# Thirty-six modulation units inside the first feed-forward, and nine row buffers for x

## The chip, the cores and the metric

The kernel runs on one core of one Trainium2 chip. The metric is the device time of one execution in microseconds (us), and lower is better.

## The reference, cut to what matters

One layer of a streaming encoder on 1152 tokens (1024 of a prompt, 8 sequences of 16 sample tokens), model width 1024, in 32-bit floating point. All sub-layers are modulated: a vector of eleven groups of 1024 numbers is computed for each of the nine sequences from its conditioning vector.

```python
def ada_mod(c, w, b, n):
    m = jax.nn.silu(c) @ w + b                 # c is (9, 1024) in all, w is (1024, n * 1024)
    return m.reshape(c.shape[0], n, D_MODEL)

def ffn_sublayer(x, mod, base, g, w1, w3, w2):
    h = modulate(rms_norm(x, g), mod[:, base], mod[:, base + 1])
    gate = 1 + mod[:, base + 2][:, None, :]
    return x + MACARON_W * gate * swiglu(h, w1, w3, w2)
```

The layer is `ffn_sublayer` with groups 0 to 2, the token mixing with groups 3 to 5, `ffn_sublayer` with groups 6 to 8, and a final norm with two more groups (9 and 10, from the weights `w_ada_f`). The feed-forward width is 2816. So the first feed-forward needs groups 0 and 1 (shift and scale) before its first product and group 2 (gate) before its first output is added to x; the other eight are needed after it.

## The kernel before, in words

The program is written engine by engine with counted semaphores; nothing is scheduled for it. SyncE (SP) issues the loads, TensorE (PE) multiplies, VectorE (DVE), ScalarE (ACT) and GpSimd (POOL) do the rest. Each engine's list of work is in the order in which the code writes it.

**Setup (lines 336 to 573).** The modulation weights are 22 halves of 512 columns (`ADA_HALVES`), each 2 MB, loaded into four buffers `ada_w`. For a half, PE does eight products that accumulate over the 1024 rows (`ada`, line 465): the stationary operand is the conditioning `cT[:, k, :]` (128 by 9), the moving one 512 columns of weights, the result is 9 partitions by 512. DVE copies it to `mod_rows` (`copy_rows`), PE turns it so that channels lie on the partitions (`turn_rows`, line 473, four small products), and DVE adds the bias into `mods` (`add_bias`). A product in plain 32-bit floats is two TensorE instructions in the trace, so a half is 16 rows of line 465 and 8 of line 473. Between the halves the nine tiles of 128 rows of x come through two buffers `x_rows` and are transposed (`turn_x`, line 456; DVE's copy is line 515). After half 15 the small states are turned, and `minus_sums` (line 303) runs over the past log gates.

**Norm (lines 575 to 678).** For three chunks of 384 tokens: squares on ACT, the sum over channels on PE (`norm_sum`, line 594), root on ACT, reciprocal (line 604) and product with x (line 612) on DVE, the modulation on DVE (line 623) and ACT (line 633), and the split of the result into a high part (`acts_hi`, ACT, line 641) and a low part (`acts_lo`, DVE, line 646), each in the format fp32r. The first norm waits for all of setup (`x_set_up`: `mod_final` 7 and `past_stored`).

**Feed-forward (`ffn_sync` to `ffn_vector`, lines 682 to 813).** Eleven pairs, each of 256 of the 2816 columns. A pair loads three blocks of 1 MB (of w1, w3, w2) into the two buffers `w_raw`; ACT and POOL split each into `w_hi` and `w_lo`. PE then does six groups of 48 products of 384 columns (banks 0 to 3, three products for each pair of operands, `mm3`), and 24 output groups of six products into banks 4 to 7; DVE adds each of the 24 to x with the gate (`add_gated`). Between the groups ACT computes the SiLU (`gated`) and DVE its product (`u_f`, line 806).

```python
            for c in range(NC):
                for d in range(KT):
                    eng.wait_ge(sem("y_free"), it * 24 + c * 8 + d - 4 + 1 + CREDIT)
```

## Time and profile before

| | |
|---|---|
| median of 3 runs | 3716.43 us (3714.55 to 3716.44) |
| span of the profiled execution | 3719.7 us |
| time around that span | none is shown beside it |
| TensorE busy | 3549.7 us, 95% of the span |
| TensorE clock, mean over the span | 0.980 of full |
| VectorE, ScalarE, GpSimd busy | 34%, 24%, 19% |
| moved from and to memory | 343.11 MB, 92 GB/s over the span |

The profile is one execution, seen by the hardware profiler. Its span runs from the first to the last instruction. In the rows below, times are microseconds unless marked ns. PE is TensorE's products, PEld its weight loads, SPq the queue that issues the loads. L465 is line 465 of the kernel. Products on TensorE are pipelined, so the distance from one start to the next says what an instruction takes, and the busy time of one is longer.

### The profile page before, as it was taken

The numbers are of one execution on the slowest core, as the hardware profiler recorded it, in microseconds if no ns is written. First come the engines' busy times: TensorE is split into PE (matmuls) and PEld (weight loads), VectorE is DVE, ScalarE is ACT, GpSimd is POOL, SyncE is SP. The second block draws the span as 40 slices with busy tenths as digits, with TensorE's granted clock in tenths as the row PEclk, the third lists the DMA queues.
The fourth block names the chain that finished last, engine by engine and source line by source line (L and its number), as shares of the span: only waits on it lengthen the run. The fifth ranks groups of instructions, "written<-read, shape, count | busy, mean of one in ns | idle before, by whom it ended". The sixth has DMA issues, their size and how long they took to land.

```text
span 3719.7 us, 53696 instructions
## 1 busy us (share of the span) xinstructions
PE 3549.7 (95%) x21007; PEld 3244.3 (87%) x21007; DVE 1276.8 (34%) x2798; ACT 909.3 (24%) x1360; POOL 705.8 (19%) x282
## 2 busy tenths in 40 slices
PE   8889999999999999999998998888999999999997
PEld 2269999999988999999998888444998999999997
DVE  1242322223256232232413766333324232223225
ACT  0031111111134232322323665222013111111112
POOL 0012322232201111111122221000111322223220
PEclk9999999999999999999999999999999999999999
DMA  8721111111111313131443333887510111111101
GB/s 303 240 76 34 45 40 50 34 42 37 57 51 61 106 65 106 48 117 54 151 146 109 89 92 82 276 279 254 194 56 28 35 44 56 34 34 45 50 18 51
DMA packets 245498, 343.11 MB, mean 92 GB/s; under 512 B 56093, under 2 KB 164053, under 8 KB 245138
## 3 DMA queue, kind: packets, MB, share of 16 engines
q1 hardware_dynamic: 218962, 308.42, 25.9%
q10 hardware_dynamic: 26432, 33.18, 2.4%
q8 instruction: 81, 1.33, 0.1%
q14 instruction: 23, 0.19, 0.0%
HBM read 293.54 MB, written 48.01 MB: 92 GB/s over the span
## 4 chain that ended last, share of the span: by engine, by line
PE 89%; DVE 3%; DMA 3%; issue 2%; ACT 2%; SPq 2%; DVEq 0%; ACTq 0%
PE psum L269 24%; PE psum L273 24%; PE psum L272 24%; PE psum L465 4%; PE psum L1412 3%; DMA kn<-k_t 2%; PE psum L1642 2%; PE psum L1392 1%; PE psum L1629 1%; PE psum L990 1%; DVE h_f L612 1%; PE psum L1379 1%; PE psum L1673 1%; PE psum L594 1%; SPq L1596 1%
## 5 line engine op out<-in xcount | busy, mean ns | idle before, releaser
L269 PE MATMUL psum<-acts_hi,w_hi 128*128 128x384 f32 x4032 | 1372.1, 340 | 29.4 <-issue 18.5
L273 PE MATMUL psum<-acts_hi,w_lo 128*128 128x384 f32 x4032 | 1359.8, 337 | 0.0
L272 PE MATMUL psum<-acts_lo,w_hi 128*128 128x384 f32 x4032 | 1359.8, 337 | 0.0
L259 POOL TENSOR_TENSOR w_lo<-w_raw,w_hi 128x2048 fp32r<-128x2048 f32 x106 | 494.1, 4670 | 1821.4 <-ACT w_hi L253 1821.4
L269 PEld LDWEIGHTS psum<-acts_hi,w_hi 128*128 128x128 f32 x4032 | 761.9, 189 | 35.6 <-issue 30.8
L272 PEld LDWEIGHTS psum<-acts_lo,w_hi 128*128 128x128 f32 x4032 | 761.8, 189 | 3.3
L273 PEld LDWEIGHTS psum<-acts_hi,w_lo 128*128 128x128 f32 x4032 | 761.5, 189 | 0.0
L806 DVE TENSOR_TENSOR u_f<-psum,gated 128x384 f32<-128x384 f32 x132 | 73.6, 558 | 994.2 <-ACT gated L761 994.2
L829 DVE SCALAR_TENSOR_TENSOR x<-psum,mods,x 128x384 f32<-128x384 f32 (+1 forms) x552 | 314.9, 570 | 194.6 <-PE psum L273 194.6
L253 ACT ACTIVATE w_hi<-w_raw 128x2048 fp32r<-128x2048 f32 x106 | 200.5, 1910 | 644.4 <-PE psum L269 606.0
L269 PE MATMUL psum<-u_hi,w_hi 128*128 128x384 f32 x1056 | 357.6, 339 | 0.0
L273 PE MATMUL psum<-u_hi,w_lo 128*128 128x384 f32 x1056 | 357.1, 338 | 0.0
L272 PE MATMUL psum<-u_lo,w_hi 128*128 128x384 f32 x1056 | 357.0, 338 | 0.0
L784 POOL TENSOR_TENSOR u_lo<-u_f,u_hi 128x384 fp32r<-128x384 f32 x132 | 134.2, 1016 | 870.4 <-ACT u_hi L763 870.4
L761 ACT ACTIVATE gated<-psum 128x384 f32<-128x384 f32 x132 | 64.9, 491 | 841.8 <-PE psum L273 841.8
L272 PEld LDWEIGHTS psum<-u_lo,w_hi 128*128 128x128 f32 x1056 | 198.5, 188 | 0.3
L269 PEld LDWEIGHTS psum<-u_hi,w_hi 128*128 128x128 f32 x1056 | 198.5, 188 | 0.3
L273 PEld LDWEIGHTS psum<-u_hi,w_lo 128*128 128x128 f32 x1056 | 198.5, 188 | 0.0
L465 PE MATMUL psum<-ada_w,cT 128*9 128x512 f32 x352 | 158.8, 605 | 14.0 <-DMA ada_w<-in_w_ada 14.0
L1412 PE MATMUL psum<-vh,pT 128*128 128x64 f32 x1152 | 146.9, 274 | 8.2 <-DVE acts_lo L1533 5.7
L1412 PEld LDWEIGHTS psum<-vh,pT 128*128 128x128 f32 x1152 | 140.8, 194 | 12.6 <-DVE acts_lo L1533 8.6
L1045 ACT ACTIVATE st<-psum 128x384 f32<-128x384 f32 x120 | 58.7, 490 | 337.6 <-PE psum L273 336.6
(224 smaller groups left out, 2880.5 us busy)
## 6 DMA issues: line engine op xcount, KB each, us to landing
w_raw<-in_ffn_w SPq DMA_DIRECT2D x66, 1024.0 KB, 5.4
ada_w<-in_w_ada SPq DMA_DIRECT2D x18, 2048.0 KB, 9.6
kc<-in_cache_k SPq DMA_DIRECT2D x16, 2048.0 KB, 10.3
vc<-in_cache_v SPq DMA_DIRECT2D x16, 2048.0 KB, 8.5
w_raw<-in_w_in SPq DMA_DIRECT2D x28, 1024.0 KB, 5.2
sp<-sample_bias SPq DMA_DIRECT2D x128, 65.0 KB, 6.7
ada_w<-in_w_ada_f SPq DMA_DIRECT2D x4, 2048.0 KB, 15.6
kf<-k_t SPq DMA_DIRECT2D x32, 256.0 KB, 4.6
```

What stands on the lines that cost most here:

```text
L253: eng.activation(w_hi[st][:], w_raw[raw][:], ACT.Copy).then_inc(sem("w_hi_done"), 1)
L259: eng.tensor_tensor(w_lo[st][:], w_raw[raw][:], w_hi[st][:].bitcast(F32), ALU.subtract).then_inc(sem("w_lo_done"), 1)
L269: pass1 = eng.matmul(out, whi, ahi, start=first, stop=False)
L272: eng.matmul(out, whi, alo, start=False, stop=False)
L273: return eng.matmul(out, wlo, ahi, start=False, stop=last)
L465: last = eng.matmul(ps[4 + slot % 2][0:NSEQ, :], cT[:, k, :], ada_w[slot][:, k, :], start=(k == 0), stop=(k == KT - 1))
L761: eng.activation(gated[n % 2][:], ps[2 * (n % 2)][:, 0:CH], ACT.Silu).then_inc(sem("gated_ready"), 1)
L784: eng.tensor_tensor(u_lo[:, t, tokens_of(c)], u_f[n % 2][:], u_hi[:, t, tokens_of(c)].bitcast(F32), ALU.subtract).then_inc(sem("u_lo_done" ...
L806: eng.tensor_tensor(u_f[n % 2][:], ps[2 * (n % 2) + 1][:, 0:CH], gated[n % 2][:], ALU.mult).then_inc(sem("u_free"), 1)
L829: last = eng.scalar_tensor_tensor(xt[:, d, t0:t0 + cp], bank[:, 0:cp], mods[:, gate, d, 0:1], xt[:, d, t0:t0 + cp], ALU.mult, ALU.add)
L1412: last = eng.matmul(ps[6 + k % 2][:, 0:HD], pT[k % 2][:, 128 * kb:128 * kb + 128], vh[hh][:, kb, :], start=(kb == 0), stop=(kb == qi))
L1642: last = eng.matmul(psum[rows, base + 512 * bk:base + 512 * bk + 512], qd[g][:, p, :], kTs[p % 2][:, 512 * bk:512 * bk + 512], start=True, ...
```

## The change

Of the 22 halves, four stay in front of the first feed-forward (groups 0 and 1). The other eighteen become 36 units of 256 columns, four in each of the first nine of the eleven pairs. A unit is loaded into `w_raw[1]`, the buffer that the w3 block uses in between. Its product is made from four column groups of the array: row block k goes to the output partitions of group k % 4, with the conditioning padded with zeros to 32 columns, and the turn sums the four groups. All nine tiles of x have a row buffer of their own and are loaded before the weights; the norm's sums stand ahead of the modulation products. The feed-forward's output groups use banks 4, 5 and 6 in place of 4 to 7 in the first feed-forward (bank 7 is for the units). The three `log1p` parts and the sums over the past log gates now stand after the norm. Several semaphores are merged.

```diff
+    FIRST = 4
+    ADA_PAIRS = 9
+    N_UNITS = 4 * ADA_PAIRS
+    def ada_product(eng, out, weights, n):
+        for k in range(KT):
+            g = k % 4
+            last = eng.matmul(out[32 * g:32 * g + 32, 0:n], cT[:, k, :], weights[:, k, :], start=(k < 4),
+                              stop=(k >= 4), skip_group_check=True)
+        last.then_inc(sem("ada_full"), 1)
+    def ada_turn(eng, out, rows, tiles):
+        for t in range(tiles):
+            last = eng.matmul(out[:, NSEQ * t:NSEQ * t + NSEQ], rows[:, 128 * t:128 * t + 128], row_sum,
+                              start=True, stop=True)
+        last.then_inc(sem("mod_turned"), 1)
...
     def setup_tensor(eng):
...
+        for c in range(NC):
+            norm_sum(eng, 0, c)
...
+        product(0)
+        product(1)
+        turn(0)
+        product(2)
+        turn(1)
+        turn(2)
+        product(3)
+        turn(3)
+
+    def setup_rest_tensor(eng):
         eng.wait_ge(sem("state_loaded"), 48)
...
+        eng.wait_ge(sem("past_summed"), 3)
...
+    def ffn1_sync(eng):
+        def unit(i, u, source):
+            if u == 0:
+                eng.wait_ge(sem("w_lo_done"), B_FFN1 + i * 3 + 1 + 1 + CREDIT)
+            eng.wait_ge(sem("ada_full"), i * 4 + FIRST + u)
+            eng.dma_start(w_raw[1][:].rearrange("p (k n) -> p k n", k=KT), source).then_inc(sem("ada_unit_loaded"), 16)
+        def pair(i, view, col, first=False):
+            ffn_load(eng, 0, i, 2)
+            if first:
+                past_store(eng)
+            unit(i, 0, view[:, :, ds(col, 256)])
+            ffn_load(eng, 0, i + 1, 0)
+            for u in range(1, 4):
+                unit(i, u, view[:, :, ds(col + 256 * u, 256)])
+            eng.wait_ge(sem("ada_full"), i * 4 + FIRST + 4)
+            ffn_load(eng, 0, i + 1, 1)
...
+    Y_BANKS = (3, 4)
...
     def ffn_tensor(eng, f):
...
+        def ada_step(i, n):
+            if n >= 1:
+                eng.wait_ge(sem("mod_rows_ready"), i * 4 + FIRST + n)
+                eng.wait_ge(sem("mod_ready"), i * 4 + FIRST + n - 1)
+                eng.wait_ge(sem("y_free"), i * 24 + CREDIT)
+                ada_turn(eng, ps[4][:, 0:2 * NSEQ], mod_part, 2)
+            if n < 4:
+                eng.wait_ge(sem("ada_unit_loaded"), i * 64 + 16 * n + 16)
+                ada_product(eng, ps[7], w_raw[1][:].rearrange("p (k n) -> p k n", k=KT), 256)
...
                     last.then_inc(sem("a_full"), 1)
+                    if ada and n < 5:
+                        ada_step(i, n)
...
-                    eng.wait_ge(sem("y_free"), it * 24 + c * 8 + d - 4 + 1 + CREDIT)
+                    eng.wait_ge(sem("y_free"), it * 24 + c * 8 + d - Y_BANKS[f] + 1 + CREDIT)
...
     def ffn_vector(eng, f):
+        def ada_step(i, n):
+            if n >= 1:
+                add_bias(eng, ps[4][:, 0:2 * NSEQ], i * 4 + FIRST + n - 1, i + 2, 2 * n - 2, 2,
+                         ds(i * 8 + 4 * FIRST + 2 * n - 2, 2))
+            if n < 4:
+                eng.wait_ge(sem("ada_full"), i * 4 + FIRST + n + 1)
+                eng.wait_ge(sem("mod_turned"), i * 4 + FIRST + n)
+                eng.tensor_copy(mod_part[:], ps[7][:, 0:256]).then_inc(sem("mod_rows_ready"), 1)
...
     def ffn_blocks_ahead(eng, f):
...
+        if f == 0:
+            eng.wait_ge(sem("ada_full"), 3)
         ffn_split_hi(eng, f, 0, 0)
+        if f == 0:
+            eng.wait_ge(sem("ada_full"), FIRST)
         ffn_split_hi(eng, f, 0, 1)
```

Where things stand in a row now. First TensorE from its first product to the feed-forward, in the kernel before, with one pass of the loop over the halves cut out (`ident,x_rows` are the transposes of x, `ident,mod_rows` the turns, `sq,ones` the norm's sums):

```order
L446 MATMUL psum<-ident,c_rows 128x9 x8
L465 MATMUL psum<-ada_w,cT 9x512 x8
...
L456 MATMUL psum<-ident,x_rows 128x128 x8
...
L465 MATMUL psum<-ada_w,cT 9x512 x8
L473 MATMUL psum<-ident,mod_rows 128x9 x8
L594 MATMUL psum<-sq,ones 128x384 x24
```

The same stretch of TensorE in the changed kernel, whole (`cols` holds the matrix that sums the four groups, `states` the padded conditioning):

```order
L479 MATMUL psum<-ident,c_rows 128x9 x8
L493 MATMUL psum<-ident,x_rows 128x128 x32
L486 MATMUL psum<-ident,vec_rows 128x88
L487 MATMUL psum<-ident,vec_rows 128x96
L493 MATMUL psum<-ident,x_rows 128x128 x40
L645 MATMUL psum<-sq,ones 128x384 x24
L455 MATMUL psum<-ada_w,states 32x512 x16
L462 MATMUL psum<-cols,mod_rows 128x9 x4
...
L526 MATMUL psum<-ident,h_rows 128x64
L528 MATMUL psum<-ident,conv_rows 128x96 x2
L533 MATMUL psum<-ident,past_rows 128x128 x8
```

The norm's sums (24 products) moved from behind the last half to ahead of the first; the past rows, which stood between halves, are now the last thing before the feed-forward.

Then VectorE of the changed kernel, from the last bias of setup to the first product of the feed-forward (`h_f` is modulated by line 682, `lam_t` are the `log1p` parts, line 309 the sums over the past log gates):

```order
L546 SCALAR_TENSOR_TENSOR mods<-mods,params 128x72
L682 TENSOR_SCALAR h_f<-h_f,mods 128x384 x5
L706 TENSOR_TENSOR acts_lo<-h_f,acts_hi 128x8x384
L682 TENSOR_SCALAR h_f<-h_f,mods 128x384 x5
L706 TENSOR_TENSOR acts_lo<-h_f,acts_hi 128x8x384
...
L601 TENSOR_TENSOR wfl_lo<-wfl_raw,wfl_hi 128x128
L603 COPY h<-psum 128x64
L604 COPY conv_state<-psum 128x192
L309 SCALAR_TENSOR_TENSOR past_rows<-ones,psum 128x512
L309 SCALAR_TENSOR_TENSOR past_rows<-ones,past_rows,psum 128x512
```

TensorE waits for the last of these (`past_summed` 3) before the first product of the feed-forward.

Last, TensorE inside a pair, at the end of the second of its six groups in the first pass of the loop:

```order
L277 MATMUL psum<-acts_hi,w_lo 128x384
...
L462 MATMUL psum<-cols,mod_part 128x9 x2
L807 REGISTER_ALU
L455 MATMUL psum<-w_raw,states 32x256 x8
L817 REGISTER_ALU
L273 MATMUL psum<-acts_hi,w_hi 128x384
```

The turn of the unit before and the product of this unit stand between two groups of 48; in the kernel before the groups follow each other with nothing between.

## Rows read from the trace of the kernel before

**Rows 1.** The page: the span, and busy time of each engine.
```profile
span 3719.7 us, 53696 instructions
...
PE 3549.7 (95%) x21007; PEld 3244.3 (87%) x21007; DVE 1276.8 (34%) x2798; ACT 909.3 (24%) x1360; POOL 705.8 (19%) x282
```
**Rows 2.** Busy time by stretch: from:to length, engines, clock, DMA share, GB/s.
```profile
0.00:217.40 217.40, 191.58 (x621) 62.09 (x621) 37.02 (x88) 10.48 (x14) 10.81 (x14) 0.98 0.73 255
217.40:242.50 25.10, 17.45 (x48) 9.89 (x48) 14.00 (x10) 15.60 (x11) 0.00 (x0) 0.84 0.00 0
242.50:321.50 79.00, 78.97 (x438) 78.98 (x439) 41.62 (x63) 22.26 (x25) 21.25 (x9) 0.97 0.13 41
321.50:397.20 75.70, 75.70 (x434) 75.70 (x433) 20.30 (x47) 11.68 (x16) 19.92 (x9) 1.00 0.13 42
```
**Rows 3.** Chain that ended last, 0 to 330: start, length, what.
```profile
5.66 7.99 DMA ada_w<-in_w_ada
...
31.20 6.96 PE psum L465 x16
38.17 0.98 PE psum L473 x8
...
234.00 2.05 DVE h_f L623 x5
236.13 2.77 ACT acts_hi L641
238.93 3.37 DVE acts_lo L646
```
**Rows 4.** Transfers, 10 to 20, by stretch as in rows 2.
```profile
10.00:20.00 10.00, 6.21 (x9) 1.13 (x10) 0.00 (x0) 0.31 (x1) 0.33 (x1) 1.00 1.05 395
```
**Rows 5.** Groups by line, 0 to 260: count, busy, mean ns, idle before.
```profile
L594 PE MATMUL psum<-sq,ones 128*128 128x384 f32 x48 | 17.4, 528 | 4.2 <-ACT sq L588 4.2
...
L515 DVE COPY x<-psum 128x512 f32 (+1 forms) x18 | 11.5, 686 | 2.8 <-PE psum L456 2.8
...
L604 DVE RECIPROCAL psum<-psum 128x384 f32<-128x384 f32 x3 | 7.7, 2561 | 10.7 <-ACT psum L600 10.7
...
L612 DVE TENSOR_TENSOR h_f<-x,psum 128x3072 f32<-128x3072 f32 x2 | 6.7, 3350 | 0.0
```
**Rows 6.** States, past sums and log1p on VectorE, by stretch as in rows 2.
```profile
171.70:178.70 7.00, 5.03 (x17) 1.67 (x18) 5.05 (x19) 0.21 (x1) 0.00 (x0) 1.00 1.05 388
```
**Rows 7.** TensorE in order of time, sample attention: start, length, group.
```profile
2419.16 0.26 PE L1652 MATMUL psum<-kn,qd 128*32 128x16 f32 x8
2419.35 1.20 PE L1662 MATMUL psum<-ident,sp 128*128 128x128 f32 x9
...
2421.59 1.95 PE L1673 MATMUL psum<-vc,spT 128*32 128x128 f32 x64 [1.05 <-DVE spT L1759]
2423.48 0.42 PE L1673 MATMUL psum<-vn,spT 16*32 16x128 f32 x8
```
**Rows 8.** TensorE in order of time, plain 32-bit products inside the projections.
```profile
1176.46 1.45 PE L990 MATMUL psum<-xc,bd 128*128 128x384 f32 x4
1177.45 0.63 PE L269 MATMUL psum<-acts_hi,w_hi 128*128 128x384 f32 x1
1177.92 0.34 PE L272 MATMUL psum<-acts_lo,w_hi 128*128 128x384 f32 x1
```
**Rows 9.** VectorE in order of time, a pair of the first feed-forward.
```profile
314.45 0.29 DVE L826 TENSOR_TENSOR s_tmp<-psum,mods 128x128 f32<-128x128 f32 x1 [0.17 <-PE psum L273]
...
346.46 0.56 DVE L806 TENSOR_TENSOR u_f<-psum,gated 128x384 f32<-128x384 f32 x1 [7.75 <-ACT gated L761]
354.85 0.56 DVE L806 TENSOR_TENSOR u_f<-psum,gated 128x384 f32<-128x384 f32 x1 [7.83 <-ACT gated L761]
```
**Rows 10.** Landing times of 1 MB blocks: inside the feed-forward, then 0 to 250.
```profile
DMA to landing us min/median/max: 4.7/5.4/8.0
...
w_raw<-in_ffn_w SPq DMA_DIRECT2D x3, 1024.0 KB, 12.4
```

More of the change, by code:

```diff
@@ L83, in program @@
     w_raw = [sb(ctx, f"w_raw{n}", [128, 2048]) for n in range(2)]
+    adaf = ExitStack()
+    ada_w = [sb(adaf, f"ada_w{n}", [128, KT, 512]) for n in range(2)]
+    adaf.close()
     w_hi = [sb(ctx, f"w_hi{n}", [128, 2048], F32R) for n in range(2)]
@@ L213, in program @@
     zf.close()
-    CONSTS = 4
+    CONSTS = 5
     NORMS_BEFORE = 3
@@ L336, in setup_sync @@
     def setup_sync(eng):
+        eng.dma_start(c_rows[0:1, :], a["c_prompt"]).then_inc(sem("c_loaded"), 16)
+        eng.dma_start(c_rows[1:NSEQ, :], a["c_sample"]).then_inc(sem("c_loaded"), 16)
+        xp = a["x_prompt"][0].rearrange("(m p) d -> m p d", p=128)
+        for tile in range(T // 128):
+            source = xp[tile] if tile < TP // 128 else a["x_sample"].rearrange("s t d -> (s t) d")
+            eng.dma_start(x_rows[tile][:], source).then_inc(sem(f"x_rows_loaded{tile // 3}"), 16)
+            if tile == 3:
+                load_vectors(eng)
@@ new lines, in load_half @@
+        def load_half(h, slot):
+            eng.dma_start(ada_w[slot][:], w_ada_v[:, :, 512 * h:512 * h + 512]).then_inc(sem(f"ada_loaded{slot}"), 16)
+        for h in range(3):
+            load_half(h, h)
+        ffn1_loads_ahead(eng)
+        eng.wait_ge(sem("ada_full"), 1)
+        load_half(3, 0)
+        eng.dma_start(state_rows[0][:], a["state_rglru"].rearrange("l s (r c) -> (l s r) c", c=128)).then_inc(sem("state_loaded"), 16)
+        conv_src = a["state_conv"].rearrange("l s j (r c) -> (l s j r) c", c=128)
@@ L455, in turn_x @@
                 for k in range(4):
-                    last = eng.transpose(ps[2 * slot + half][:, 128 * k:128 * k + 128],
-                                         x_rows[slot][:, 512 * half + 128 * k:512 * half + 128 * k + 128], ident[:])
+                    last = eng.transpose(ps[tile % 2 * 2 + half][:, 128 * k:128 * k + 128],
+                                         x_rows[tile][:, 512 * half + 128 * k:512 * half + 128 * k + 128], ident[:])
                 last.then_inc(sem("x_turned"), 1)
-        def ada(h, slot, loads):
-            eng.wait_ge(sem(f"ada_loaded{slot}"), 16 * loads)
-            for k in range(KT):
-                last = eng.matmul(ps[4 + slot % 2][0:NSEQ, :], cT[:, k, :], ada_w[slot][:, k, :],
-                                  start=(k == 0), stop=(k == KT - 1))
-            last.then_inc(sem("ada_full"), 1)
@@ L487, in setup_tensor, with product, turn @@
-        turn_x(0, TP // 128, TP // 256 + 1)
+        eng.wait_ge(sem("params_ready"), 1)
+        for c in range(NC):
+            norm_sum(eng, 0, c)
+        def product(h):
+            eng.wait_ge(sem(f"ada_loaded{h % 3}"), 16 * (h // 3 + 1))
+            if h >= 2:
+                eng.wait_ge(sem("mod_rows_ready"), h - 1)
+            ada_product(eng, ps[START_BANKS[h % 2]], ada_w[h % 3], 512)
+        def turn(h):
+            eng.wait_ge(sem("mod_rows_ready"), h + 1)
+            if h >= 1:
+                eng.wait_ge(sem("mod_ready"), h)
+            ada_turn(eng, ps[4][:, TURN_AT], mod_rows[h % 2], 4)
@@ L495, in setup_tensor @@
         for half in range(2):
[L496 removed]
             for k in range(4):
[L498 removed]
+                last = eng.transpose(ps[1 + half][:, 128 * k:128 * k + 128], past_rows[:, 4 * half + k, :], ident[:])
             last.then_inc(sem("states_turned"), 1)
[L500 to L503 removed]
+        eng.wait_ge(sem("past_summed"), 3)
@@ L538, in setup_vector, with copy_rows @@
-        move_x(0, TP // 128)
+                eng.tensor_copy(x[:, 4 * half:4 * half + 4, 128 * tile:128 * tile + 128],
+                                ps[tile % 2 * 2 + half][:].rearrange("p (k n) -> p k n", k=4)).then_inc(sem("x_moved"), 1)
+        for c in range(NC):
+            norm_inverse(eng, 0, c)
+            norm_times_inverse(eng, 0, c)
+        def copy_rows(h):
+            eng.wait_ge(sem("ada_full"), h + 1)
+            if h >= 2:
+                eng.wait_ge(sem("mod_turned"), h - 1)
+            eng.tensor_copy(mod_rows[h % 2][:], ps[START_BANKS[h % 2]]).then_inc(sem("mod_rows_ready"), 1)
@@ L650, in norm_scalar @@
     def norm_scalar(eng, n, x_ready):
-        for c in range(NC):
-            x_ready(eng, c)
-            norm_square(eng, n, c)
-            if c >= 1:
-                norm_root(eng, n, c - 1)
+        if n > 0:
+            for c in range(NC):
+                x_ready(eng, c)
+                norm_square(eng, n, c)
+                if c >= 1:
+                    norm_root(eng, n, c - 1)
         if n < 3:
@@ new lines, in ffn1_loads_ahead @@
+    def ffn1_loads_ahead(eng):
+        ffn_load(eng, 0, 0, 0)
+        ffn_load(eng, 0, 0, 1)
+    def ffn1_sync(eng):
[14 more added lines that the diff above has]
+            ffn_load(eng, 0, i + 1, 1)
+        pair(0, w_ada_v, 2 * D, first=True)
+        with eng.Fori(1, NMOD - 4) as i:
+            pair(i, w_ada_v, i * D + 2 * D)
+        with eng.Fori(0, 2) as i:
+            pair(i + (NMOD - 4), w_adaf_v, i * D)
+        with eng.Fori(ADA_PAIRS, FF_PAIRS - 1) as i:
+            ffn_load(eng, 0, i, 2)
+            ffn_load(eng, 0, i + 1, 0)
+            ffn_load(eng, 0, i + 1, 1)
+        ffn_load(eng, 0, FF_PAIRS - 1, 2)
@@ L1976, in _ @@
         setup_tensor(eng)
-        for c in range(NC):
-            norm_sum(eng, 0, c)
+        setup_rest_tensor(eng)
         ffn_tensor(eng, 0)
```

384 lines of the change are left out of this document (195 added, 189 removed).

## The prediction

> **What bounds the kernel now.** I read the page first: TensorE is busy for 95% of the span [rows 1]. A share is an average, so the second view is the busy time by stretch [rows 2]. For 217.4 us TensorE computes the modulation, then 25.1 us of norm follow with no transfer at all, and the first product of the feed-forward stands at 242.5. A pair then takes 75.7 us (the first one 79.0), with TensorE full and the transfers at 0.13. The third view, the chain of waits [rows 3], shows what fills the front: a half is 6.96 us of products (16 instructions, 0.435 us each for 512 columns, or 0.85 ns a column) and 0.98 us of turns, and 22 x 7.94 = 175 us of the 217 are that. The result has nine rows, so this is TensorE time spent on streaming weights past a nearly empty array. A half of 2 MB needs 5.3 us at 395 GB/s [rows 4], less than its 7.94: the front is bound by TensorE, not by memory.
>
> So two questions decide: how much earlier the feed-forward starts, and what a unit costs inside pairs where TensorE has no idle time.
>
> **What a product of four column groups costs.** The sample attention already has this form [rows 7]: 64 instructions of 128 columns, four groups in turn, have their successor 1.89 us later, 29.5 ns each, where 0.85 ns a column would give 109. They run beside each other, 3.7 times faster. A unit is 8 products, 16 instructions of 256 columns: 16 x 218 / 3.7 = 0.94 us. One of the four halves in front takes 1.88 us. The turn of a unit is four instructions at 0.98 / 8 = 0.12 [rows 3]: 0.49 us.
>
> The Trainium skill (TensorE: Matmul & The Clock Gate, the table of measured packing) gives 2.38 times for three column groups. Scaled to four that would be 3.2, an estimate from that page, and 5 us more over the 36 units. The measured row decides, since it is this form on this engine.
>
> **The start, added up.** Loads: the first 2 MB took 7.99 us from issue [rows 3], of which 5.3 are the transfer, so 2.7 us are latency. Three tiles of x (1.6 MB, 4 us) land at about 8, all nine (12 us) at 16. VectorE copies a tile in 2 x 0.686 [rows 5]: from 8.5, nine tiles and the parameters end at 21. The three sums take 17.4 us on TensorE [rows 5] and run from 20.6 to 38. VectorE then is the one that is late. Its reciprocal and product are 2.56 + 3.35 a chunk [rows 5], from 28.5 for three chunks to 46.4, and only then does it copy the first half (0.69 for this form, as for x) at 47.1. Halves 0 and 1 were multiplied by 41.5, so TensorE waits 5.6 us. From 47.1 come, in turn, four turns (4 x 1.0), two products (2 x 1.9, some of it at the lower clock, which TensorE also had after its wait in the norm, mean 0.84 [rows 2]; 5.3 together), two copies (1.4) and the small steps: 58.4. Half 3 is loaded when product 0 is done, at 40 + 8 = 48, before it is needed.
>
> Then chunk 0 is modulated, rounded and subtracted: 2.05 + 2.77 + 3.37 [rows 3], with the hops to 67.2, and chunk 1 behind it to 76. Before, TensorE started right behind chunk 0. Now it waits for the past sums, which stand behind chunk 1 on VectorE: their whole group was 5.05 us busy [rows 6], here 5.7 with ScalarE's logarithm in it. **The feed-forward starts at 81.7 and not at 242.5: 160.8 us earned.** For the bounds: 72, if VectorE keeps closer to the loads and the hops are short; 95, if the small loads (64-byte pieces) or the table loads of ScalarE come late.
>
> **What the pairs pay.** Four units are 4 x (0.94 + 0.49) = 5.7 us a pair, and all of it lies on the path, since TensorE is full there [rows 2]. On top comes the break in the stream, five a pair. Four plain 32-bit instructions of 384 columns between fp32r products [rows 8] move the stream by 1177.92 - 1176.46 - 0.17 = 1.29, of which 4 x 384 x 0.85 ns = 1.30 are their own streaming: a break costs nothing. By the second row alone it costs 0.3 (0.47 to the next start instead of 0.17). I take 0.15, between them: 45 x 0.15 = 6.8, with 0 and 13.5 kept as ends. Nine pairs: 51.5 + 6.8 = 58.
>
> The Trainium skill (TensorEngine Tiling (Array Packing), Tiling Modes) speaks against this change: a change of the tiling mode drains the engine. The row says less. Eight column-group products and the full-width ones behind them start 0.19 us apart [rows 7], no room for a drain of any size. By the rule, an estimate from it with what a product has in flight (0.34 long, 0.17 apart) for 72 switches, it would be 12 us more.
>
> **What waits, pair by pair.** A unit is loaded when the product before is done. The groups of 48 are 8.39 us apart [rows 9] (354.85 - 346.46), so with the turn there are 9.0 us. A 1 MB block in the same 1 KB pieces lands after 5.4 us, at most 8.0 [rows 10]: no wait. SyncE's queue is strict, and the load for w1 of the next pair stands ahead of unit 1. It waits for GpSimd's split of w2, which is done 6 us into the pair, so it holds nothing up. w3 of the next pair now starts after unit 3, some 40 us into the pair, lands at 46, and is split after the last group at 59: late by nothing. On VectorE a step adds a copy and a bias, about 0.7 us, where it sat idle for 7.8 [rows 9]. Three output banks for four: at its busiest VectorE still waits 0.17 us for TensorE at each output group [rows 9], so two banks in flight are enough. Nothing is paid.
>
> In the first pair VectorE modulates chunk 2 behind the second group and waits for ScalarE in it; the copy of unit 1 comes about 2.3 us after TensorE wants it. That is 2.5 us, once. The store of the past sums (0.5 MB) has 10 us to land before ScalarE's first SiLU needs its space.
>
> **The sum.** 58 + 2.5 - 160.8 = -100 against the span of 3719.7. The median of the runs is 3.3 us below that span and I take the difference to stay: 3716.4 - 100.0 = 3616 us. Ends: start 72 and free breaks give -170.5 + 51.5 = -119, 3597. Start 95, breaks of 0.3 and 8 us of waits in the first pairs give -147.5 + 65 + 8 = -74.5, 3642.
>
> **Rivals.**
> - *Units land late.* Each of 27 loads (units 1 to 3) has 9.0 us. In setup, with other loads in the queue, 1 MB took 12.4 us [rows 10]. At 10 us: 27 x 1.3 = 35, so 3652. At 12.4: 27 x 3.7 = 100, so 3717. For it: the traffic inside a pair grows from 3 to 7 MB. Against it: the share is 0.13 now, and the loads come one at a time. 7% for some of it, 1% for all.
> - *The column groups don't overlap* beside fp32r work with 256 columns. Then a unit's product is 3.49 us and not 0.94: 36 x 2.55 = 92. Four halves in front cost 5.1 us more each, less the 5.6 idle: 15. With breaks of 0.3: 7. Together 114 - 100 = +14, 3730, slower than before. The point from which it decides: slower when a unit costs over 4.4 us in all. Against it stands the row of the sample attention. 4%.
> - *The start does not shrink as the sum says:* VectorE's chain or the small loads put it beyond 100. Then 18 us and more are lost, 3635 to 3650. 10%, inside the range.
> - *The change doesn't do what it says,* with SyncE's queue holding the units behind a block that waits for the pair's end: then each pair would stall for tens of us. The order of the queue shows no such block. Under 1%.
>
> **How the numbers follow.** 78% for the forecast as added up, 10% for the late start, 8% for late units, 4% for groups one after another. The range 3597 to 3652 takes in the ends of the sum, the late start and the landing of 10 us; some 12% lies outside. A measurement of this kernel can tell 0.2%, 7.4 us, from no change. Slower by more is the 4% rival, within 0.2% is the full landing time, 2% with its neighbours, and faster is the rest.
>
> **What would show it.** In the profile of the changed kernel: the first feed-forward product at 72 to 95, with TensorE waiting on VectorE twice before it (copy of the first half, past sums); the three sums ahead of the modulation; steps of 16 instructions in 0.9 to 1.0 us in the units; pairs 0 to 8 at 81 to 84 us, pairs 9 and 10 still at 75.7; no wait on a unit's load; and everything behind the first feed-forward as long as it was. Wrong would be: unit products at 3.5 us, waits of TensorE on `w_raw`, pairs over 86, or a start past 100.

## The result and the profile after

| | before | after |
|---|---|---|
| median of the runs on the same chip | 3715.49 us (3712.62 to 3716.44, 4) | 3626.96 us (3621.44 to 3627.85, 4) |
| span of the profiled execution | 3719.7 us | 3625.7 us |
| first product of the first feed-forward | 242.5 | 84.1 |
| first `u_f` of the first feed-forward | 254.14 | 95.52 |
| last `u_f` of the first feed-forward | 1052.56 | 951.45 |
| first to last product with `vc` (sample attention) | 2352.9 to 2605.5 | 2253.2 to 2512.7 |

The ratio is 0.976, 95% interval 0.9746 to 0.9774: 88.5 us faster, 94.0 by the spans. 3616 was forecast.

The page of the changed kernel, as in [rows 1]:
```profile
span 3625.7 us, 54412 instructions
...
PE 3439.9 (95%) x21295; PEld 3232.4 (89%) x21295; DVE 1283.6 (35%) x2835; ACT 910.2 (25%) x1360; POOL 704.2 (19%) x283
```
TensorE has lost 109.8 us of work and the same share of a shorter span is left. Busy time by stretch, columns as in [rows 2] (the stretches are setup with the norm, pair 0, pair 1, and two pieces of the first two):
```profile
0.00:83.90 83.90, 43.87 (x237) 28.43 (x237) 52.77 (x65) 30.89 (x29) 11.16 (x15) 0.81 0.63 204
83.90:171.30 87.40, 84.52 (x500) 80.87 (x501) 27.48 (x54) 17.17 (x20) 20.24 (x9) 0.93 0.32 103
171.30:252.70 81.40, 81.40 (x514) 78.75 (x513) 22.20 (x55) 11.63 (x15) 19.93 (x9) 1.00 0.28 90
60.00:80.00 20.00, 0.00 (x0) 0.00 (x0) 13.95 (x22) 12.51 (x14) 1.99 (x1) 0.50 0.09 37
116.00:130.00 14.00, 12.96 (x71) 11.67 (x71) 2.05 (x6) 0.52 (x1) 1.00 (x1) 0.76 0.24 76
```
In front TensorE now is busy for half the time, and for the last 20 us not at all: a chain on VectorE and ScalarE has taken its place as the bound. A steady pair is 81.4 with TensorE full, at a DMA share of 0.28. The first pair is 5.8 longer.

The front, from the chain of waits (start, length, what):
```profile
41.40 3.35 DVE h_f L660
44.75 0.61 DVE mod_rows L576
45.41 1.88 PE psum L462 x8
...
57.57 4.52 DVE mods L546
62.12 2.04 DVE h_f L682 x5
64.24 2.77 ACT acts_hi L701
...
72.44 2.77 ACT acts_hi L701
75.23 3.36 DVE acts_lo L706
...
82.39 1.29 DVE past_rows L309
```
L576 is the copy of the first half behind all three norm chunks, L309 the past sums. L546 turns a scale into its final form; the same operation takes 0.23 us in experiments 7 and 10, and here it lasted 4.5. TensorE in order of time: first setup, then in pair 0 the turn of unit 1 with the product of unit 2, and one such step of pair 1:
```profile
20.53 15.65 PE L645 MATMUL psum<-sq,ones 128*128 128x384 f32 x48
36.11 3.64 PE L455 MATMUL psum<-ada_w,states 128*32 128x512 f32 x32
...
84.13 0.68 PE L273 MATMUL psum<-acts_hi,w_hi 128*128 128x384 f32 x1 [25.20 <-DVE past_rows L309]
...
117.04 1.03 PE L462 MATMUL psum<-cols,mod_part 128*128 128x9 f32 x4 [2.65 <-DVE mod_part L929]
118.00 1.94 PE L455 MATMUL psum<-w_raw,states 128*32 128x256 f32 x16
...
211.24 0.51 PE L462 MATMUL psum<-cols,mod_part 128*128 128x9 f32 x4
211.68 1.07 PE L455 MATMUL psum<-w_raw,states 128*32 128x256 f32 x16
```
A steady turn takes 0.44 us (211.68 - 211.24) and a unit's product about 1.07. In pair 0 TensorE waits 2.65 us for the copy of unit 1 and then runs at twice these times. VectorE in order of time shows the pair's rhythm, one group of 48 products with turn and product each, then the output groups:
```profile
192.24 0.56 DVE L938 TENSOR_TENSOR u_f<-psum,gated 128x384 f32<-128x384 f32 x1 [8.57 <-ACT gated L884]
...
202.06 0.56 DVE L938 TENSOR_TENSOR u_f<-psum,gated 128x384 f32<-128x384 f32 x1 [8.62 <-ACT gated L884]
...
211.96 0.56 DVE L938 TENSOR_TENSOR u_f<-psum,gated 128x384 f32<-128x384 f32 x1 [8.62 <-ACT gated L884]
```
9.90 us where [rows 9] had 8.39: a unit with its turn and all its breaks costs 1.51. The output groups of the kernel after, and in the second block of rows of the kernel before:
```profile
154.99 0.62 DVE L971 SCALAR_TENSOR_TENSOR x<-psum,mods,x 128x384 f32<-128x384 f32 x1 [0.42 <-PE psum L277]
156.03 0.62 DVE L971 SCALAR_TENSOR_TENSOR x<-psum,mods,x 128x384 f32<-128x384 f32 x1 [0.42 <-PE psum L277]
```
```profile
300.72 0.62 DVE L829 SCALAR_TENSOR_TENSOR x<-psum,mods,x 128x384 f32<-128x384 f32 x1 [0.44 <-PE psum L273]
301.78 0.62 DVE L829 SCALAR_TENSOR_TENSOR x<-psum,mods,x 128x384 f32<-128x384 f32 x1 [0.44 <-PE psum L273]
```
They stand 1.040 us apart, before 1.056 (means over the first feed-forward, and the same in the second, which the change does not touch). That is 24 x 0.016 = 0.38 us a pair for nothing that was asked for.

**Where 94.0 us come from.** To the first `u_f` -158.6; pair 0 +11.6 (87.20 for 75.64); the next eight +46.2 (81.43 for 75.66); the last stretch -0.2. To the last `u_f` that is -101.1. Behind it the program lost 7.1: 2674.2 us from there to the end, before 2667.1. Most of that lies in the sample attention. First the transfers into `kc`, by the page of after, then of before (KB each, median us to landing):
```profile
kc<-in_cache_k SPq DMA_DIRECT2D x16, 2048.0 KB, 10.9
```
```profile
kc<-in_cache_k SPq DMA_DIRECT2D x16, 2048.0 KB, 10.3
```
Then busy time from the first to the last product with `vc`, of after, of before, and of the kernel of experiment 12, columns as in [rows 2]:
```profile
2253.20:2512.70 259.50, 216.93 (x2092) 124.87 (x2092) 89.94 (x221) 63.52 (x116) 0.00 (x0) 0.93 0.87 261
```
```profile
2352.90:2605.50 252.60, 215.28 (x2090) 122.22 (x2092) 89.94 (x221) 63.46 (x116) 0.00 (x0) 0.94 0.85 268
```
```profile
2352.10:2594.40 242.30, 207.85 (x2092) 118.13 (x2092) 89.95 (x221) 63.52 (x116) 0.00 (x0) 0.98 0.88 279
```
The stage took 259.4 us, before 252.6. Transfers (0.87) and TensorE (84% busy) are both near their full share, so the rows do not say which of them paces it. Its length goes with the granted clock: 0.93, 0.94 and 0.98.

### The profile page after: what moved, and what is told of

Same layout as the page of the kernel before. It is cut to its first block, busy times and chain, and to the rows that moved or that the text cites. A ratio compares the mean times of both kernels' runs of the same rounds, so it can differ in the third digit from the quotient of the medians.

```text
span 3625.7 us, 54412 instructions
## 1 busy us (share of the span) xinstructions
PE 3439.9 (95%) x21295; PEld 3232.4 (89%) x21295; DVE 1283.6 (35%) x2835; ACT 910.2 (25%) x1360; POOL 704.2 (19%) x283
## 4 chain that ended last, share of the span: by engine, by line
PE 88%; DVE 4%; DMA 3%; issue 2%; ACT 2%; SPq 1%; DVEq 0%; ACTq 0%
PE psum L273 25%; PE psum L277 25%; PE psum L276 24%; PE psum L1554 3%; DMA kn<-k_t 2%; PE psum L1784 2%; PE psum L1534 2%; PE psum L1771 1%; PE psum L455 1%; DVE h_f L660 1%; PE psum L1132 1%; PE psum L1521 1%; PE psum L1815 1%; SPq L1738 1%; PE psum L1522 1%
## 5 line engine op out<-in xcount | busy, mean ns | idle before, releaser
L273 PE MATMUL psum<-acts_hi,w_hi 128*128 128x384 f32 x4032 | 1375.9, 341 | 50.3 <-DVE past_rows L309 25.2
L263 POOL TENSOR_TENSOR w_lo<-w_raw,w_hi 128x2048 fp32r<-128x2048 f32 x106 | 492.1, 4650 | 1628.5 <-ACT w_hi L257 1628.5
L1601 ACT ACTIVATE pr<-pr,stat 128x128 f32<-128x128 f32 (+7 forms) x128 | 98.8, 772 | 51.1 <-DVE stat L1655 50.0
## 6 DMA issues: line engine op xcount, KB each, us to landing
kc<-in_cache_k SPq DMA_DIRECT2D x16, 2048.0 KB, 10.9
```

Of the source, the lines that this page charges most:

```text
L263: eng.tensor_tensor(w_lo[st][:], w_raw[raw][:], w_hi[st][:].bitcast(F32), ALU.subtract).then_inc(sem("w_lo_done"), 1)
L273: pass1 = eng.matmul(out, whi, ahi, start=first, stop=False)
L1601: eng.activation(pr[k % 4][:, 0:keys], pr[k % 4][:, 0:keys], ACT.Exp, bias=stat[:, k % 4, 1:2], accum_out=stat[:, k % 4, 2:3]).then_inc(se ...
```

## The experiments

All against the kernel before on the same chip. "First `u_f`", "pair" (interval from one pair's first `u_f` to the next one's) and "attention" (first to last product with `vc`) are from the profiled execution. A time "less than the change" compares two medians; where the runs were made on another chip, the kernel before took 3716.2 to 3717.9 us there, and 3715.49 where the change was measured. By the intervals such a difference is good to some 5 or 6 us.

### 1 and 2. Addresses

Both odd effects sit in code that the change does not touch. What it did touch is addresses: it merges the small tiles of before (`eps_col`, `past_last` and others) into one, `cols`, and every large tile behind it (x, `u_hi`, `u_lo`, `kc`, `vc`) now starts 64 bytes lower in each partition. The first kernel takes that back, the second makes the same edits without the 64 bytes.

```diff
-    cols = sb(ctx, "cols", [128, 24])
+    cols = sb(ctx, "cols", [128, 40])
...
+    partf = ExitStack()
+    mod_part = sb(partf, "mod_part", [128, 256])
+    partf.close()
...
-    mod_part = sb(ffnf, "mod_part", [128, 256])
...
+                if n == 0:
+                    eng.wait_ge(sem("y_free"), i * 24 + CREDIT)
```
(`mod_part` now lies over `s_tmp`, hence the wait. The second kernel keeps 24 columns.)

> The changed kernel with 64 bytes a partition added to its small tile of columns, so that every tile behind it (x, u_hi, u_lo, the third weight buffers, the buffers of both attentions) lies at the address it had before the change, and with mod_part laid over s_tmp to make room. Theory A (the addresses explain what the stages behind the first feed-forward give back): output groups of both feed-forwards 1.056 us apart again, not 1.040 (+8 us over 22 pairs), and the sample attention gets back the 7 us that it lost; both together about 0 to -5 us against the change. Theory B (chance from run to run): output groups and sample attention as in the change, 3627 us. The first feed-forward starts at 84 in both.

Measured: 3620.09 us (3617.73 to 3632.15), ratio 0.9742 [0.9729, 0.9756]. Output groups 1.056 apart in both feed-forwards, pairs 81.94, attention 249.1, `kc` lands in 10.0. The profiled execution is the slowest of the five.

> The control of the run before: mod_part laid over s_tmp as there, but no bytes added, so all addresses are those of the change. Both theories: 3627 us, output groups 1.040 us apart, sample attention as in the change. If this differs from the change, the new wait for y_free costs something and the pair of runs is read against each other.

Measured: 3626.18 us (3623.61 to 3626.74), ratio 0.9758 [0.9744, 0.9771]. Groups 1.040, pairs 81.42, attention 254.5, `kc` 10.7. The two kernels are the same but for 64 bytes, and the groups follow them: 1.056 or 1.040, in both feed-forwards. The attention is less clear. Eight traces have the addresses of the change (after and experiments 2, 4, 5, 6, 7, 8, 10), and their attention took 252.0 to 259.8 us, so the 5.4 us between experiments 1 and 2 are not shown by this pair alone. What keeps apart in every trace is the landing of `kc`: 10.7 to 11.0 in those eight, 10.0 to 10.3 in experiment 1 and in before. By the medians the kernel of experiment 1 is 6.1 us faster than that of 2, though its feed-forwards are slower.

### 3. The kernel before, shifted

```diff
+    sb(ctx, "gap", [128, 16])
```

> The kernel before the change with one unused tile of 64 bytes a partition among its small tiles, so that all later tiles lie 64 bytes higher. Nothing else differs. Theory A (addresses matter): the output groups go from 1.056 to about 1.040 us (-8 us), and the sample attention loses 5 to 10 us, near 3715 in all. Theory B (they don't): 3715.5 us with both stages as before.

Measured: 3711.34 us (3701.09 to 3716.25, 11 runs; before 3716.24 in 15), ratio 0.9986 [0.9977, 0.9995]. Groups 1.040 and pairs 75.04 (75.66 before), attention 256.2, `kc` 10.9. The tile moves everything behind it 64 bytes up, and it does to the groups and to `kc` what 64 bytes down did. The pairs gain 0.62, of which the groups are 0.38; the groups of 48 products gave the rest (8.35 us apart for 8.39). What the median gained, 4.9, is less than 22 pairs of 0.62, so some of it was lost behind them, as the 256.2 for 252.6 of the attention suggest.

### 4. One column group

```diff
-            g = k % 4
-            last = eng.matmul(out[32 * g:32 * g + 32, 0:n], cT[:, k, :], weights[:, k, :], start=(k < 4),
-                              stop=(k >= 4), skip_group_check=True)
+            last = eng.matmul(out[0:32, 0:n], cT[:, k, :], weights[:, k, :], start=(k == 0), stop=(k == KT - 1))
```
(turns and copies then take 32 rows.)

> The changed kernel with all eight products of a half or unit in one column group (output partitions 0 to 31), accumulated over k, and the turn over these 32 rows alone. Theory of the prediction (the four groups run beside each other): a unit's 16 instructions take 3.4 us and not 0.94, pairs 0 to 8 are 91.3 us and not 81.4 (+89 us), the start is some 14 us later, 3725 to 3735 us in all. Rival (the groups bring nothing, the small cost has another cause): 3627 us.

Measured: 3735.75 us (3733.62 to 3738.04), ratio 1.0052 [1.0036, 1.0067], slower than before. First `u_f` 107.19, pairs 92.48. TensorE in order of time:
```profile
211.23 0.61 PE L460 MATMUL psum<-cols,mod_part 32*128 32x9 f32 x4
211.77 3.64 PE L454 MATMUL psum<-w_raw,states 128*32 128x256 f32 x16
```
3.64 us for the product that takes 1.07 in four groups, and 11.05 more for a pair. This is the rival that was to end on the other side, made real: it gives 3736 where 3730 was worked out for it. The groups do run beside each other, and the change lives by them: without them it is a loss.

### 5. The past sums earlier

TensorE's last wait in front is for L309, behind chunk 1 on VectorE, though VectorE sits idle for ScalarE before chunk 0's lower part. The edit puts the two scans there and the `log1p` parts behind both chunks.

```diff
         norm_scale(eng, n, 0)
+        if n == 0:
+            past_sums(eng)
```

> The changed kernel with VectorE's copies of the states and the sums over the past log gates put right behind the modulation of chunk 0, in the 2.9 us in which VectorE waits for ScalarE's rounding, and TensorE waiting for these two sums alone. Theory (the past sums are what holds the first feed-forward): it starts right behind acts_lo of chunk 0, at 70 to 72 and not 84, and the kernel is 12 to 13 us faster, 3614. Rival (the loads or GpSimd's split are just as late): it starts past 78, less than 6 us gained.

Measured: 3613.32 us (3609.44 to 3619.2), ratio 0.9726 [0.9709, 0.9743], 13.6 less than the change. VectorE, then TensorE, in order of time:
```profile
67.74 1.22 DVE L309 TENSOR_TENSOR_SCAN past_rows<-ones,psum 128x512 f32<-128x512 f32 x1
69.08 1.28 DVE L309 TENSOR_TENSOR_SCAN past_rows<-ones,past_rows,psum 128x512 f32<-128x512 f32 x1
```
```profile
74.06 0.68 PE L273 MATMUL psum<-acts_hi,w_hi 128*128 128x384 f32 x1 [10.14 <-DVE acts_lo L709]
...
97.62 1.94 PE L455 MATMUL psum<-w_raw,states 128*32 128x256 f32 x16 [3.76 <-DMA w_raw<-in_w_ada]
```
The start is 10.1 us earlier (74.1, where 70 to 72 were expected). A wait of 3.76 us for unit 1's load has taken the place of the one of 2.65 for its copy. Even so, from the first product to the first `u_f` of pair 1 it took 97.4 us for 98.6.

### 6. The copy of unit 1 first

```diff
+                if ada and n < 5:
+                    ada_step(i, n)
                 if first_step and n == 1:
                     norm_scale(eng, 2 * f, 2)
                     norm_lo(eng, 2 * f, 2)
-                if ada and n < 5:
-                    ada_step(i, n)
```

> The changed kernel with VectorE's step for unit 1 (bias and copy) ahead of the modulation of chunk 2 in the first pair. Theory (TensorE's wait of 2.6 us for that copy also costs it its full clock for some 3 us): the first pair falls from 87 to about 82 us between its first u_f and the next pair's, 5 to 6 us gained, 3621. Rival (only the wait counts): 2.6 us. Another (the modulation of chunk 2 becomes late instead): nothing.

Measured: 3621.65 us (3618.97 to 3630.57), ratio 0.9751 [0.9733, 0.9769], 5.3 less. Pair 0 took 81.52 for 87.20.
```profile
117.16 0.51 PE L462 MATMUL psum<-cols,mod_part 128*128 128x9 f32 x4
117.59 1.07 PE L455 MATMUL psum<-w_raw,states 128*32 128x256 f32 x16
```
The 5.3 alone would be at the edge of what medians show; the 5.68 of pair 0 are read in the trace. With the 2.65 us of wait gone, the clock stayed up as well, and that was the other half of the loss. But the second half is not bound to the wait. The trace of experiment 9 has the same wait without it:
```profile
116.99 0.61 PE L465 MATMUL psum<-cols,mod_part 128*128 128x9 f32 x4 [2.62 <-DVE mod_part L934]
117.53 1.07 PE L458 MATMUL psum<-w_raw,states 128*32 128x256 f32 x16
```
There the granted clock is 1.00 over 116 to 130, and pair 0 took 84.55, 3.0 over a steady pair and not 5.8. Of six traces with this wait (after, 1, 2, 7, 9, 10) five show the lower clock behind it.

### 7 and 10. The 4.5 us of L546

While L546 lasted, GpSimd ran its second weight split (L263). The first edit holds that split until the scale is final, the second until VectorE has modulated chunk 0.

```diff
         for j in range(2):
+            if (f, j) == (0, 1):
+                eng.wait_ge(sem("mod_final"), 1)
             split_lo(eng, block0 + j, FFN_SLOTS[j])
```

> The changed kernel with GpSimd's split of the second weight block waiting for VectorE's scale of the modulation (mod_final). Theory (the scale, two inputs in SBUF, was held for 4.3 us until GpSimd's running split of 128 x 2048 ended, an exclusive port): the scale takes 0.23 us and not 4.51, all behind it is 4.3 us earlier, the feed-forward starts at 79.6, 3623 us. Rival (it was held by something else, such as the first use of a form): it stays at 4.5 us and nothing is gained.

Measured: 3628.65 us (3622.37 to 3630.86), ratio 0.9764 [0.9747, 0.978], no gain. VectorE, then GpSimd:
```profile
60.89 0.23 DVE L546 SCALAR_TENSOR_TENSOR mods<-mods,params 128x72 f32<-128x72 f32 x1
61.16 6.33 DVE L682 TENSOR_SCALAR h_f<-h_f,mods 128x384 f32<-128x384 f32 x5
```
```profile
61.20 4.51 POOL L263 TENSOR_TENSOR w_lo<-w_raw,w_hi 128x2048 fp32r<-128x2048 f32 x1 [3.47 <-DVE mods L546]
```
The scale is short again, and the same 4.3 us now stand in the five operations behind it (6.33 for 2.03): the first of the five lasts until GpSimd is done. From the start of L546 to the first product it is 26.6 us, as in the change. The first product itself stands at 87.5, 3.4 us later than there, and that is not from the edit: the fourth product of setup ran at the lower clock (3.62 us for 1.90). So it did in experiments 1 and 6, which leave the front as it is and start at 87.5 and 86.6.

```diff
+                eng.wait_ge(sem("h_ready"), 1)
```

> The changed kernel with GpSimd's second weight split held until VectorE has modulated the first chunk (both the final scale and the five operations behind it then have no GpSimd operation beside them; the split falls into the wait of VectorE for ScalarE's upper part). If VectorE's 4.51 us for an operation of 0.23 us is the port that the two engines share, the scale takes 0.23 us, the five behind it 2.0 us together and the first product of the feed-forward starts 2 to 4.3 us earlier than in the changed kernel: 3623 to 3625 us. If it is anything else (a wait that the trace puts down wrongly), the scale stays at 4.5 us and nothing changes: 3627 us.

Measured: 3628.82 us (3624.28 to 3630.03), ratio 0.976 [0.9746, 0.9774], no gain. VectorE, then TensorE:
```profile
58.69 0.23 DVE L546 SCALAR_TENSOR_TENSOR mods<-mods,params 128x72 f32<-128x72 f32 x1
58.97 2.04 DVE L682 TENSOR_SCALAR h_f<-h_f,mods 128x384 f32<-128x384 f32 x5
63.90 4.93 DVE L706 TENSOR_TENSOR acts_lo<-h_f,acts_hi 128x3072 fp32r<-128x3072 f32 x1 [2.89 <-ACT acts_hi L701]
```
```profile
82.57 0.68 PE L273 MATMUL psum<-acts_hi,w_hi 128*128 128x384 f32 x1 [21.63 <-DVE past_rows L309]
```
Both are short now, and `acts_lo` pays 1.6 (4.93 for 3.36), since the split ran from 61.09 to 65.61. From the start of L546 to the first product it is 23.9 us for 26.6, which is the 4.3 less the 1.6, and within the 2 to 4.3 expected. The start is only 1.6 us earlier, because setup was late again for the clock (2.92 us for its fourth product). The cause is confirmed; what its removal is worth, 2.7 us, is too little for the medians to show.

### 8. Early sums, and the first copy ahead of the last norm chunk

```diff
-        for c in range(NC):
+        for c in range(NC - 1):
             norm_inverse(eng, 0, c)
             norm_times_inverse(eng, 0, c)
...
         norm_lo(eng, n, 0)
+        if n == 0:
+            norm_inverse(eng, 0, 2)
+            norm_times_inverse(eng, 0, 2)
```
(on top of 5, with TensorE's first turn waiting for the last root.)

> The past sums early as in the run before the last, and VectorE's copies of the first two halves ahead of the reciprocal and product of chunk 2, which go behind acts_lo of chunk 0. Theory (TensorE's wait of 5.7 us for the first copy then vanishes): the third and fourth products of setup come 4 to 6 us earlier unless the load of half 3 binds them, the feed-forward starts at 65 to 67, 16 to 19 us faster than the change, 3608 to 3611. Rival (half 3 lands too late, at 47 to 50): only 1 to 3 us beyond the early sums.

Measured: 3614.27 us (3610.7 to 3616.65), ratio 0.972 [0.9704, 0.9736], no better than 5. The start is at 66.3, as expected, but the last `u_f` stands at 939.75, in 5 at 940.14. TensorE, then GpSimd, then SyncE's queue:
```profile
96.09 1.94 PE L455 MATMUL psum<-w_raw,states 128*32 128x256 f32 x16 [9.08 <-DMA w_raw<-in_w_ada]
```
```profile
82.72 4.61 POOL L263 TENSOR_TENSOR w_lo<-w_raw,w_hi 128x2048 fp32r<-128x2048 f32 x1 [25.24 <-ACT w_hi L257]
```
```profile
87.35 0.37 SPq L249 DMA_DIRECT2D w_raw<-in_ffn_w  x1
87.77 10.69 SPq L773 DMA_DIRECT2D w_raw<-in_w_ada  x2
```
What the front gained became a wait of 9.08 us. Unit 1's load stands behind the next pair's w1 load, that one waits for GpSimd's split of w2, and the split waits for ScalarE, whose work for the norm and the `log1p` parts stands ahead of it. The prediction's sentence on this queue ("it holds nothing up") holds only while the copy of unit 1 is late anyway.

### 9 and 12. Which tile

The first adds to 1 a gap ahead of the two parts of the feed-forward product alone, the second adds that gap to the kernel before and nothing else.

```diff
     ffnf = ExitStack()
+    sb(ffnf, "u_gap", [128, 16])
     u_hi = sb(ffnf, "u_hi", [128, 2, T], F32R)
```

> The changed kernel with all tiles behind the small columns back at their old addresses (as in the run with the old addresses), and one gap of 64 bytes ahead of the two parts of the feed-forward product, so that these alone lie 64 bytes off their old place while the attention's buffers lie on it. If the output groups' 1.040 us (1.056 at the old addresses) hang on where the product's parts lie, the groups are 1.040 apart again, pairs last 81.4 us and the first attention for the samples 249 to 253 us (kc landing in 10.0 to 10.3 at the median): 3612 to 3619 us. If they hang on x's place or on another tile's, groups stay at 1.056 and pairs at 81.9, and the time is that of the run with the old addresses, about 3620 us.

Measured: 3614.83 us (3607.49 to 3618.68), ratio 0.9727 [0.9713, 0.9741]. Groups 1.040, pairs 81.57, attention 244.1, `kc` 9.9.

> The kernel before with one unused tile of 64 bytes per partition ahead of the two parts of the feed-forward product, and nothing else: x and the attention's buffers lie where they lay. If the groups' 1.040 us come from where the product's parts lie, all 22 pairs have groups 1.040 apart instead of 1.056, 0.38 us less each, 8 us in all, and the pairs of the first feed-forward last 75.3 us: 3706 to 3711 us. If also the shorter first attention (244 us in the two runs with this gap and the old addresses, 249 to 253 without the gap) comes from it, 3698 to 3705 us. If the groups hang on another tile, nothing changes: 3716 us.

Measured: 3707.78 us (3704.73 to 3710.63, 8 runs; before 3716.46 in 12), ratio 0.9975 [0.9965, 0.9986]. Groups 1.040, pairs 75.29, attention 242.3, `kc` 10.1. The median gained 8.7 where 22 x 0.38 = 8.4 was worked out. So `u_hi` and `u_lo`'s place sets the groups' distance: the gap also moves `gated`, `u_f` and `s_tmp`, but the products that set it read only these two. `kc` is back at its old place and lands as it did there (9.9 and 10.1). That the attention was shorter than 249 in the three traces with the gap (9, 11 and 12) is not explained by any tile that it uses, and the median of 12 leaves no room for much of it. What these three share is TensorE's clock in that stage, 0.98 of full, where the eleven others have 0.93 to 0.96. Why it stayed up, no run shows.

### 11. All of it

Experiments 5, 6, 8, 9 and 10 together, and in pair 0 unit 1's load ahead of the next w1 load:

```diff
+            if first:
+                unit(i, 1, view[:, :, ds(col + 256, 256)])
             ffn_load(eng, 0, i + 1, 0)
-            for u in range(1, 4):
+            for u in range(2 if first else 1, 4):
```

> All that the single runs showed to be worth something, in one kernel: old addresses with the 64 byte gap, past sums ahead of the feed-forward's waits, the last norm chunk behind the copy of the first half, the first pair's copy of unit 1 ahead of the last norm chunk, the weight split held until the first chunk is modulated, and unit 1's load issued ahead of the next pair's first weight load (it waited 9 us behind that one where the sums and the copy were both early). If the parts add up: feed-forward's first product at 62 to 68 us, first pair 82 to 84 us, output groups 1.040 apart, attention 249 to 253 us: 3590 to 3602 us. If the first pair again waits for unit 1's load (what the early start gains is then a wait for a transfer), it lasts 86 us or more and the time is 3603 to 3612 us.

Measured: **3586.5 us (3583.2 to 3589.27), ratio 0.9649 [0.9636, 0.9662]**, 131 us under before and 40 under the change, and faster than expected. TensorE, then the stretches of pair 0 (its first part) and of a steady pair:
```profile
61.87 0.68 PE L276 MATMUL psum<-acts_hi,w_hi 128*128 128x384 f32 x1 [6.89 <-DVE acts_lo L714]
```
```profile
61.90:139.00 77.10, 77.10 (x471) 74.45 (x472) 35.89 (x59) 23.10 (x27) 20.94 (x9) 0.96 0.32 103
...
155.40:237.00 81.60, 81.60 (x520) 78.94 (x512) 22.30 (x55) 11.62 (x15) 19.89 (x9) 1.00 0.28 90
```
The start is 22.3 us earlier than in the change, pair 0 has no wait, and the last `u_f` is at 925.19 for 951.45. The first copy moved ahead of the norm is worth its time once the load behind it is not late. Behind the last `u_f` another 18.0 us are gone (2656.2 for 2674.2), 15.7 of them in the attention, at a clock of 0.98 for 0.93; how much of that the addresses did stays open.

## Why the prediction was right, and where it was off

**What bounds and what is removed: right.** TensorE streams all 22 halves as before, but over four column groups, so that a half's products cost it about 2 us and not 6.96 (1.90 in front, two units of 1.00 from one start to the next in a pair). Experiment 4 shows the other side: with one group the same order of work is 109 us dearer.

**The start: -160.8 forecast, -158.4 by the first product (84.1 for 242.5), and that close because two errors cancel.** The norm's sums took 15.65 us and not 17.4, the copy of the first half was done at 45.4 and not at 47.1 (of which 0.2 are a slip of the sum: 28.5 + 3 x 5.91 is 46.2, not 46.4). Against that stood 4.3 us that no step had: VectorE's L546, held until GpSimd was done. The "past sums behind chunk 1" were seen (81.7), and experiment 5 shows that they were worth 10 us of start. Some luck was in it too: with the same front, experiments 1 and 6 start 3.4 and 2.5 us later, by the clock in setup.

**A pair: 6.48 forecast, 5.77 measured.** A turn 0.44 (forecast 0.49), a product with its breaks 1.07 (forecast 0.94, and 0.15 for a break). A unit in all is 1.51, from 9.90 - 8.39. Four of them are 6.04, and the pair's unit steps together 6.15; the groups' 0.38 comes off that. With nothing for breaks the sum gave 5.72, so 0.43 is left for five breaks, 0.09 each. With the addresses of before on both sides the difference is read directly: 81.94 in experiment 1 for 75.66 is 6.28, and then it is 0.11 each. The rate of 3.7 and the break can't be told apart from this. By the Trainium skill (TensorE: Matmul & The Clock Gate, the table of measured packing), scaled from three groups to 3.2 for four (an estimate), a product is 1.09 and the breaks are nothing. Here 3.64 for one group against 1.07 is 3.4, breaks in. By the rule of the Trainium skill (TensorEngine Tiling (Array Packing), Tiling Modes), that a change of the mode drains the engine, it would have been 12 us over the units by the prediction's estimate. The trace agrees with little of it: all that could be called a break is 9 x 0.43 = 4 us, or 5 by experiment 1.

**What waits: the first pair was mis-sized, the rest right.** No unit waited for its load in a steady pair (landing 5.0 and 5.5 at the median), three banks cost nothing. In pair 0 the wait was 2.65 us, forecast 2.3. But the term "+2.5, once" was 5.8, and pair 0 went past the 86 us that were to be a sign of error: the granted clock fell to half behind the wait (0.76 over 116 to 130), and experiment 6 got both back at once. The step counted the wait and put its effect on the clock at nothing. In the trace of experiment 9, where the clock held, the term was 3.0. In the rival of late units the sums use 8.7 us of room (27 x 1.3, 27 x 3.7) where the text gives 9.0; by 9.0 they are 27 and 92 us, and nothing else changes.

**"Everything behind the first feed-forward as long as it was": the step that failed.** It was 7.1 us longer in the two traces. The step looked at instructions and not at addresses, and took one execution to be like the next. Two effects of addresses are shown. The output groups gain 22 x 0.38 = 8.4 us (experiments 1 to 3, 9 and 12). And `kc` lands in 9.9 to 10.3 us at its old place (five traces), in 10.7 to 11.0 with it 64 bytes off (nine traces). The attention was 242 to 253 us in the first five and 252 to 260 in the nine. But this length also goes with the granted clock, and in the eight traces with the addresses of the change the part behind the last `u_f` was anything from 2665.0 to 2679.2 us (before 2667.1, experiment 1 2670.1). So how much of the 7.1 is addresses and how much is the one execution stays open.

**From the span to the median.** -101.1 at the last `u_f` against -100.0 forecast, a match by luck: the start 2.2 short, pair 0 3.3 dearer, the units 6.4 cheaper, the end 0.2 shorter. Then +7.1 behind it; and the profiled execution of before was 4.2 us above its median, that of after 1.3 below (by the spans), where the difference was taken to stay: 5.5. Together -88.5. Since the trace of before was a long execution, what is read from it behind the feed-forward may be long as well. The rivals of late units and a late start did not occur.

## What to carry to other kernels

A product with few result rows belongs in column groups before it is moved anywhere: moved in one group, the weights cost 20 us against the kernel before (experiment 4), in four groups they gained 88. When TensorE's front work is moved away, draw the other engines' chain that is left, in order, with the queue of loads beside it: 26 of the 44 us that experiment 11 found (by the spans) lay ahead of the last `u_f`, most of them in which small operation or load stood behind which. And when a change moves addresses, compare stages that it does not touch, and run the old kernel with an unused tile before explaining a few us by anything else. Do it with several traces: at the same addresses the attention spread over 8 us.

## What the runs showed of the hardware

- **64 bytes in a tile's start.** Groups of six products stand 1.056 us apart with `u_hi` and `u_lo` at their old place, 1.040 with them 64 bytes off in either direction, in every profile (176.0 and 173.3 ns from one product to the next). Transfers of 2 MB into `kc` landed in 9.9 to 10.3 us (medians) at its old place and in 10.7 to 11.0 with it 64 bytes off. Why, no run shows.
- **VectorE against GpSimd.** A SCALAR_TENSOR_TENSOR of 0.23 us took 4.51 and a TENSOR_SCALAR of 0.47 took 4.77 until GpSimd's 4.5 us split ended; experiment 10 has 1.6 more on a TENSOR_TENSOR. The Trainium skill (SBUF — State Buffer, the section on SBUF's two separate sides) has this as a pair of ports that the two share by an exclusive lock, for VectorE's operations in a mode that uses both ports, or with two inputs in SBUF against a GpSimd operation that reads SBUF, as the split does. The first and the last row have two such inputs and agree; for the TENSOR_SCALAR, with one tensor, it would be such a mode, which no row here shows by itself. In experiment 7 the rows have VectorE's operation start at 61.16 and the split at 61.20, and it was VectorE's that was held.
- **A short wait can cost twice.** Behind 2.65 us without work TensorE's granted clock was at its lower level (1.2 GHz) until about 123.2, 6.1 us after TensorE began again, and the products were 0.32 us apart for 0.17. So it went in five traces; in the sixth, of experiment 9, the clock held behind 2.62 us without work. Behind the wait of 25.2 us in front it was low until 89.0, 4.9 us after the start.
- **The clock differs between executions of one code.** In setup the fourth of the modulation products took 1.90 us in the traces of after and of experiment 9, and 3.62 in those of experiments 1, 6 and 7. In the sample attention the mean was 0.93 where it took 259.4 us, 0.94 where it took 252.6 and 0.98 where it took 242.3.
